# Gate halo of the first FFN block: tokens stationary in four column groups, then a 0/1 product

## The reference, cut to what matters

```python
def _conv_glu(h, w_gate, w_up, ffn_conv_w, ffn_conv_b, w_down):
    gate = _causal_dwconv(h @ w_gate, ffn_conv_w) + ffn_conv_b
    return (jax.nn.silu(gate) * (h @ w_up)) @ w_down
```

## Time and profile before

| | us |
|---|---|
| median of 3 runs | 3988.8 |
| lowest and highest run | 3984.1, 3991.41 |
| span of the profiled execution | 3987.5 |
| PE busy | 3396.2 (85%) |
| DVE busy | 1812.8 (45%) |
| ACT busy | 1269.7 (32%) |
| mean granted PE clock | 0.921 |

### The profile page before, as it was taken

How to read it: one execution, slowest core, us unless ns; L and a number is a source line. 1 busy time by engine, 2 the same in 40 slices (tenths; PEclk the granted TensorE clock), 3 DMA queues, 4 the chain that set the end, 5 groups by cost and what they waited for, 6 DMA issues and landing times. The chain is left out here.

```text
span 3987.5 us, 51409 instructions
## 1 busy us (share of the span) xinstructions
PE 3396.2 (85%) x17935; PEld 2846.2 (71%) x17935; DVE 1812.8 (45%) x2733; ACT 1269.7 (32%) x2352; POOL 677.0 (17%) x918
## 2 busy tenths in 40 slices
PE   7986759965777677899993995999999999999998
PEld 6865559964666664666762774887788878887887
DVE  2115514434555634665564772443255335524542
ACT  3214512223333311444443332433133223322331
POOL 1113400006655610000002551000000000010000
PEclk9998879987888888899996997999999999999999
DMA  5433452222222236302102564333433343344323
GB/s 168 144 126 98 116 202 65 64 54 75 80 73 71 84 120 194 111 27 65 58 17 98 177 195 152 84 84 122 146 102 95 126 138 99 85 155 124 97 81 105
DMA packets 406340, 426.55 MB, mean 107 GB/s; under 512 B 33850, under 2 KB 324102, under 8 KB 404310
## 3 DMA queue, kind: packets, MB, share of 16 engines
q1 hardware_dynamic: 367270, 319.06, 26.9%
q0 software_dynamic: 26240, 91.67, 7.3%
q10 hardware_dynamic: 12720, 14.42, 1.1%
HBM read 299.97 MB, written 125.10 MB: 107 GB/s over the span
## 5 line engine op out<-in xcount | busy, mean ns | idle before, releaser
L2161 DVE TENSOR_TENSOR ff_w_lo<-ff_w_raw,ff_w_hi 128x2048 fp32r<-128x2048 f32 (+1 forms) x176 | 309.3, 1759 | 577.7 <-ACT ff_w_hi L2126 577.7
L2126 ACT ACTIVATE ff_w_hi<-ff_w_raw 128x2048 fp32r<-128x2048 f32 (+1 forms) x176 | 261.9, 1488 | 500.7 <-PE ff_pD L2241 347.3
L2219 PE MATMUL ff_pG<-ff_u_hi,ff_w_hi 128*128 128x512 f32 x704 | 278.4, 395 | 33.2 <-DVE ff_w_lo L2161 33.2
L2241 PE MATMUL ff_pD<-ff_w_hi,ff_g_hi 128*128 128x512 f32 x704 | 275.8, 392 | 8.4 <-DVE ff_w_lo L2161 4.9
L2219 PE MATMUL ff_pG<-ff_u_lo,ff_w_hi 128*128 128x512 f32 x704 | 277.1, 394 | 0.0
L2219 PE MATMUL ff_pG<-ff_u_hi,ff_w_lo 128*128 128x512 f32 x704 | 276.8, 393 | 0.0
L2219 PE MATMUL ff_pU<-ff_u_hi,ff_w_hi 128*128 128x512 f32 x704 | 276.7, 393 | 0.0
L2241 PE MATMUL ff_pD<-ff_w_lo,ff_g_hi 128*128 128x512 f32 x704 | 275.1, 391 | 0.0
L2241 PE MATMUL ff_pD<-ff_w_hi,ff_g_lo 128*128 128x512 f32 x704 | 274.9, 391 | 0.0
L2219 PE MATMUL ff_pU<-ff_u_hi,ff_w_lo 128*128 128x512 f32 x704 | 274.5, 390 | 0.0
L2219 PE MATMUL ff_pU<-ff_u_lo,ff_w_hi 128*128 128x512 f32 x704 | 274.3, 390 | 0.0
(11 more groups left out here) (342 smaller groups left out, 7729.5 us busy)
## 6 DMA issues: line engine op xcount, KB each, us to landing
ff_w_raw<-in_w_gate SPq DMA_DIRECT2D x88, 512.0 KB, 3.9
ff_w_raw<-in_w_up SPq DMA_DIRECT2D x88, 512.0 KB, 5.1
ff_w_raw<-in_w_down SPq DMA_DIRECT2D x176, 256.0 KB, 2.8
scr_prod<-dn_out SPq DMA_DIRECT2D x17, 1280.0 KB, 4.6
sn_prod<-scr_prod SPq DMA_DIRECT2D x33, 640.0 KB, 4.1
dn_qkv<-scr_dtok SPq DMA_DIRECT2D x68, 192.0 KB, 3.9
scr_dtok<-cv_ob SPq DMA_DIRECT2D x12, 1024.0 KB, 5.3
scr_tok<-pj_tok POOLq DMA_DIRECT2D x17, 548.0 KB, 3.1
```

The costliest lines, as they stand in the source:

```text
L2126: act.activation(w_hi[s][:, 0:w], w_raw[s][:, 0:w], ACT.Copy).then_inc(w_half[s], 1)
L2161: dve.tensor_tensor(w_lo[s][:, 0:w], w_raw[s][:, 0:w], f(w_hi[s][:, 0:w]), ALU.subtract).then_inc(w_ready[s], 1)
L2219: m = pe.matmul(bank[s][:, :], a[s][:, o:o + P], x[:, k, :], start=(k == 0 and n_pass == 0), stop=(k == KD - 1 and n_pass == 2))
L2241: m = pe.matmul(pD[t][:, :], x[:, ft, t * P:t * P + P], a[s][:, i * 512:i * 512 + 512], start=(ft == 0 and n_pass == 0), stop=(ft == FT - ...
```

## The change

The two halo tokens become the stationary operand. `head` is widened to 32 columns (two tokens, then zeros that POOL writes first). Each of the 8 slices goes to one of four groups of 32 array columns (j = k % 4), with the 128 raw gate weights of the slice as the moving operand, so `pD[s][32j:32j+32, 0:128]` holds four partial sums with tokens on the partitions. These matmuls now stand ahead of pG, at the head of the unit. ACT copies the 128 x 128 partial sums to `head_part[s]`. After pG, PE multiplies `head_part` with `pick`, a matrix of zeros and ones that POOL makes once out of the identity: this adds the four groups and turns the result, into `pD[s][:, 128:130]`, where ACT's copy reads it.

```diff
         @block.gpsimd
         def _(pool):
+            pool.memset(head[:, :, :], 0.0).then_inc(zeroed, 1)
             make_identity(pool, ident, id_made)
+            pool.wait_ge(id_made, 2)
+            pool.tensor_tensor(pick[:, 0, :], ident[:, 0:HW], ident[:, HW:2 * HW], ALU.add).then_inc(picked, 1)
+            pool.tensor_tensor(pick[:, 1, :], ident[:, 2 * HW:3 * HW], ident[:, 3 * HW:], ALU.add).then_inc(picked, 1)
+            pool.wait_ge(picked, 2)
+            pool.tensor_tensor(pick[:, 2, :], pick[:, 0, :], pick[:, 1, :], ALU.add).then_inc(picked, 1)
...
                 def gate(t, s, c):
+                    if isinstance(b, int):
+                        act.wait_ge(head_done[s], c + 1)
+                        act.activation(head_part[s][:, :], pD[s][:, 0:P], ACT.Copy).then_inc(head_out[s], 1)
                     act.wait_ge(gate_done[s], c + 1)
...
             dve.wait_ge(consts, 64)
-            dve.tensor_tensor(head[:, :, :], head_hi[:, :, :], head_lo[:, :, :], ALU.add).then_inc(head_ready, 1)
+            dve.wait_ge(zeroed, 1)
+            dve.tensor_tensor(head[:, :, 0:HALO], head_hi[:, :, :], head_lo[:, :, :], ALU.add).then_inc(head_ready, 1)
...
             pe.wait_ge(head_ready, 1)
+            pe.wait_ge(picked, 3)
...
                     pe.wait_ge(w_ready[s], u + 1)
+                    if isinstance(b, int):
+                        pe.wait_ge(gate_out[s], c)
+                        for k in range(KD):
+                            j = k % HG
+                            m = pe.matmul(pD[s][j * HW:j * HW + HW, 0:P], head[:, k, :], w_raw[s][:, k * P:k * P + P],
+                                          start=(k < HG), stop=(k >= KD - HG), tile_position=(0, j * HW))
+                        m.then_inc(head_done[s], 1)
...
                         if i == 0 and isinstance(b, int):
-                            for k in range(KD):
-                                m = pe.matmul(pD[s][:, 0:HALO], w_raw[s][:, k * P:k * P + P], head[:, k, :],
-                                              start=(k == 0), stop=(k == KD - 1))
+                            pe.wait_ge(head_out[s], c + 1)
+                            m = pe.matmul(pD[s][:, P:P + HALO], head_part[s][:, :], pick[:, 2, 0:HALO], start=True, stop=True)
                         m.then_inc(done[s], 1)
```

More of the change, by code:

```diff
@@ L1999, in stage_ffn @@
         taps = r.sb("taps", [P, (TAPS + 1) * FT])
+        HG, HW = 4, P // 4
         head_hi = r.sb("head_hi", [P, KD, HALO])
         head_lo = r.sb("head_lo", [P, KD, HALO])
-        head = r.sb("head", [P, KD, HALO])
+        head = r.sb("head", [P, KD, HW])
+        head_part = [r.sb(f"head_part{i}", [P, P]) for i in range(2)]
+        pick = r.sb("pick", [P, 3, HW])
         halo = r.sb("halo", [P, FT, HALO])
@@ L2016, in stage_ffn @@
         halo_used = r.sems("halo_used")
+        zeroed, picked, head_done, head_out = r.sem("zeroed"), r.sem("picked"), r.sems("head_done"), r.sems("head_out")
         conv_step, convolved, active, g_made, g_half, g_ready = (
@@ L2132, in gate @@
                     act.activation(gb[s][:, HALO:B], pG[s][:, 0:B - HALO], ACT.Copy)
-                    before = pD[s][:, 0:HALO] if isinstance(b, int) else halo[:, bass.ds(t, 1), :].rearrange("p a n -> p (a n)")
+                    before = pD[s][:, P:P + HALO] if isinstance(b, int) else halo[:, bass.ds(t, 1), :].rearrange("p a n -> p (a n)")
                     act.activation(gb[s][:, 0:HALO], before, ACT.Copy).then_inc(halo_used[s], 1)
```

## The result

The changed kernel takes 4040.1 us (median of 4 runs, 4039.75 to 4041.98) against 3988.4 us before in the same comparison: a ratio of 1.0126, 95% interval [1.0111, 1.0140]. The profiled execution took 4041.98 us with a span of 4040.3 us, 52.8 us above the span before. The forecast was 4045 us.

The account below looks back on a forecast made before the run. PE was taken to bound the kernel before; after the change, a loop of waits through load and ACT. 38 - 1.4 + 0.5 = +37 us, plus 19 for the clock, makes 56 on 3987.5: 4045 us forecast, range 4025 to 4066.

Parts of the forecast that it names:

- The ring: Block 0, units 1 to 20: load, w_hi, head copy, pick, pU wait on each other in a closed loop; +38 us.
- The clock: Block 0: PE's clock falls behind the new idle, slowing pU; twelve falls at about 1.6 us, +19 us.
- the clock holds: Rival for block 0: short idles don't lower PE's clock, only 37 us remain, 4026 us; chance 0.10.
- in every unit: Rival for block 0: the clock falls in every unit, 71 us, 4060 us, up to 4068 with later landings; chance 0.10.
- PE's own sum: Block 0: head work on PE 1.06 us in place of 1.79, a gain of 0.7 us per unit if nothing waits.
- the changes of shape: On PE in each unit of block 0: switching the array's shape in and out, 0.4 us together (bounds 0.2 and 0.6).
- the stage's start: POOL's memset and three small additions ahead of its loads at the start; +0.5 us (bounds 0 and 1.2).
- The other side: Rival for block 0: the copy is done before pG ends and the tiling pays, 0.7 us per unit, 3973 us; chance 0.04.
- The faster rival: Block 0: the transfer lands by about E + 4.4 (E: previous unit's last pU matmul starts), tiling pays, 3973 us; chance 0.04.

Follow-up runs that it names:

- e4: The changed kernel plus 7 never-read matmuls of 512 columns per unit of block 0, between pG and PE's wait for ACT; 4020.2 us, ratio 1.0088.
- e1: The changed kernel with ACT's copy into head_part moved ahead of its split of the next unit's weights, block 0 only; 3970.1 us, ratio 0.9946.
- e2: The changed kernel with SP's load in block 0 waiting for the head matmuls (head_done), not for the unit's end (unit_done); 3968.0 us, ratio 0.9941.
- e3: The kernel before plus only the wait: in block 0 PE waits before pU for an unused ACT copy at the head of gate; 4050.2 us, ratio 1.0153.
- e5: e1 with all 8 slices in one group of 32 columns instead of four; ratio 1.0016 to the kernel before, units of 13.25 us.
- e7: e1 with the two tokens padded by zeros to 128 stationary columns, so the array's shape never changes; ratio 1.0003 to the kernel before.
- e8: The kernel before plus 5 never-read float32 products (20 instructions) on PE during its wait at the start of the stage; ratio 0.9993.

## Why the prediction was right

*The ring.* Predicted even units 13.98 us; measured 13.8 to 14.0 in the nine where the clock held. Predicted odd units 15.27 us before the clock; e4 shows 15.2 to 15.4 where the clock held. Predicted PE idle "some 47 us together", from 1.7 and 3.0 us; measured 48.0 us, 1.68 and 3.02. e1 and e2 show that it takes both the copy's place behind `split` and the load's wait for `unit_done`; e3 shows that the wait by itself makes the loss.

*The clock.* Twelve falls at 1.6 us, +19 us, were a count by nearness to two rows; it was eleven, at 7.2 - 5.6 = 1.6 us, 17.7 us. The price came from the pG at 3616.43, before which PE had idled 4.84 us, longer than here, and held all the same. That the count came so near is partly luck: it went by the length of the idle, and e3 has falls behind 0.78 to 1.26 us, where this kernel has none behind 1.59 to 1.76. The rival "the clock holds" is refuted by the 0.50 behind each odd unit, and "in every unit" by nine pU of 5.6 us. The Trainium skill, page "TensorE: Matmul & The Clock Gate", section "Loop structure matters more than you think", has bursts with waits between them run cold; the rows agree for the ten waits of about 3 us, and disagree for nine of the ten shorter ones, of about 1.7 us.

*PE's own sum.* Predicted a gain of 0.7 us, units of 12.0 us, where nothing waits: unit 21 and all of e1 have 12.0. The 0.44 us for four groups held (0.57 us on the chain, one entry into the shape included), the changes of shape were over-sized, 0.28 us for both instead of 0.4, and so small that nothing hung on it. The Trainium skill, page "TensorEngine Tiling (Array Packing)", section "Theoretical Speedup", gives up to 4x for a small dimension of 32 or less; 0.11 against 0.025 us per instruction is about that, with the assumed tail. The swap by itself, e5 and e7, was a loss of 10.9 and 5.0 us.

*The whole.* Predicted +56 us; the span rose by 52.8. Its parts: 4.4 us lie ahead of this stage, where nothing was changed, and belong to the scatter; the stage's start and unit 0 gave -0.4 us (predicted +0.5 and -0.7; measured +0.65 up to PE's first matmul and -1.0 in the unit); units 1 to 21 +55.3 us (predicted 38 + 19 - 0.7 = 56.3); behind block 0 -6.5 us, 6.1 of it ahead of block 1. The last is the one term that my sum lacked. It has nothing to do with the halo's work: 20 more instructions of PE ahead of it moved a fetch of 16 KB in e8 and brought the same gain, and in all ten profiles the long wait goes with a fetch at this place. That the fetch is what delays the loads was not tried apart from that. The median (4040.1) lies 5 us under the forecast (4045); that this is no more is in part luck, since the profiled execution also has 4.4 us ahead of the stage, which no term foresaw.

*The other side.* The faster rival asked for a transfer that lands early enough. It did not come by itself, but e2 brought it about, and the kernel then took 3968 us where that rival had 3973; units of 12.0 us bear out its 0.7 us per unit, and the rest is the time behind block 0 and scatter, which it did not name.

## What to carry to other kernels

Before a product is made cheaper by sending its partial sums through another engine, look at what stands ahead of that copy in the engine's queue, and at what that in turn waits for; here a 0.26 us copy stood behind a transfer that PE itself had to release. Cut the loop at either link: put the copy first in the queue, or let the load wait for the last reader of its buffer and not for the end of the whole unit. When an engine idles for two or three microseconds on the path that sets the time, count the idle time and then the slower clock behind it; here the second added almost half of the first. Don't take a shorter idle for harmless either: in e3 the clock fell behind 0.78 us.

## What the runs showed of the hardware

Four groups of 32 columns ran float32 matmuls of 128 moving columns side by side (0.11, 0.053 and 0.025 us per instruction with one, two and four groups), and entering and leaving the shape cost 0.28 us together. Useless matmuls in idle time shortened a stretch by 13.5 us: the clock fell twice instead of eleven times. The clock held behind nine idle times of 1.59 to 1.76 us in one kernel and fell behind 0.78 us in another, so their length alone doesn't decide. And 20 unused instructions at the start of a stage shortened a way of 133 us, some 300 us later, by 5.8 us: a fetch of instructions fell earlier, PE's wait for a load shrank from 4.90 to 0.68 us, and the clock behind it held.
